# Half of each conditioning block weighed by TensorE, and first operands of two stages loaded one stage ahead

## What the kernel must compute

```python
mod = c @ w_ada[l] + b_ada[l]                  # c: 1 x 1024, w_ada: 1024 x 6144
sh_a, sc_a, gt_a, sh_f, sc_f, gt_f = jnp.split(mod[:, None, :], 6, axis=-1)
h = rmsnorm(x, norm_mix[l]) * (1.0 + sc_a) + sh_a
x = x + gt_a * hybrid_mixer(h, w_in[l], w_conv[l], ...)   # h @ w_in, convolution, gated delta rule, attention
h = rmsnorm(x, norm_ffn[l]) * (1.0 + sc_f) + sh_f
x = x + gt_f * hierarchical_moe(h, ...)
```

## Time and profile before

| | us |
|---|---|
| median of 3 runs | 2518.68 (2518.53 to 2520.19) |
| the profiled execution, its own time | 2507.53 |
| its span in the profile | 2505.4 |
| TensorE busy in the span | 2206.2 (88%) |
| VectorE, ScalarE, GpSimd busy | 1126.5, 922.0, 382.8 |
| mean granted TensorE clock | 0.949 of full speed |

### The profile page before, as it was taken

The page is one execution under the profiler, slowest core; times in us unless marked ns, Lnnn a source line. Parts: engine busy times, 40 slices in busy tenths (PEclk is TensorE's granted clock), DMA queues, the critical chain, the costliest instruction groups (busy, mean ns, idle before and its releaser), DMA issues. The chain is left out here.

```text
span 2505.4 us, 33260 instructions
## 1 busy us (share of the span) xinstructions
PE 2206.2 (88%) x9964; PEld 1242.9 (50%) x9965; DVE 1126.5 (45%) x2294; ACT 922.0 (37%) x2136; POOL 382.8 (15%) x320
## 2 busy tenths in 40 slices
PE   3999899999988897897999998878885998999990
PEld 2666544444444445896777774444552333333330
DVE  5444222232233752555888775656652222222223
ACT  1333111111233311224778774323323443444433
POOL 0000000000011101344333110010012222222220
PEclk9999999999999998998999999988887999999995
DMA  8444102211255544985223324343354988989747
GB/s 341 147 153 147 50 34 90 104 59 50 99 173 178 182 178 131 311 261 200 89 92 105 102 89 162 127 119 99 121 210 148 306 261 284 328 249 312 218 80 287
DMA packets 178320, 418.13 MB, mean 167 GB/s; under 512 B 41192, under 2 KB 81000, under 8 KB 162744
## 3 DMA queue, kind: packets, MB, share of 16 engines
q1 hardware_dynamic: 155944, 346.59, 39.6%
q0 software_dynamic: 13472, 45.26, 7.8%
q10 hardware_dynamic: 8816, 25.18, 2.9%
HBM read 296.84 MB, written 124.85 MB: 168 GB/s over the span
## 5 line engine op out<-in xcount | busy, mean ns | idle before, releaser
L644 PE MATMUL ps<-big,pc_w 128*128 128x512 f32 x1280 | 558.0, 597 | 10.6 <-DMA pc_w<-in_w_chan 10.6
L644 PEld LDWEIGHTS ps<-big,pc_w 128*128 128x128 f32 x1280 | 243.9, 192 | 312.3 <-issue 300.9
L2108 PE MATMUL ps<-big,ex_xt 128*64 x672 | 302.2, 603 | 2.1 <-ACT ex_xt L2151 2.1
L2109 PE MATMUL ps<-ex_wgu,ex_xt 128*64 128x512 f32 x672 | 302.2, 603 | 0.0
L1621 PE MATMUL ps<-w_out,mo_yt 128*128 128x512 f32 x512 | 235.5, 619 | 0.0
L309 PE MATMUL ps<-cp_wt,big 128*128 128x344 f32 x768 | 225.4, 454 | 0.0
L2159 ACT COPY ex_wgu<-big 128x4096 f32 x43 | 155.1, 3607 | 84.7 <-SPq L2025 51.9
L309 PEld LDWEIGHTS ps<-cp_wt,big 128*128 128x128 f32 x768 | 145.8, 191 | 76.9 <-issue 4.0
L1363 PE MATMUL ps<-at_v,at_pt 128*128 128x128 f32 (+1 forms) x1200 | 182.8, 290 | 0.0
L1429 ACT ACTIVATE at_p<-at_p,at_low 128x256 f32<-128x256 f32 (+1 forms) x384 | 174.0, 456 | 19.1 <-DVE at_low L1392 18.8
L2108 PEld LDWEIGHTS ps<-big,ex_xt 128*64 128x64 f32 x672 | 89.7, 139 | 181.1 <-issue 181.1
(11 more groups left out here) (295 smaller groups left out, 3187.8 us busy)
## 6 DMA issues: line engine op xcount, KB each, us to landing
big<-in_w_gate_up SPq DMA_DIRECT2D x32, 2048.0 KB, 11.2
ex_wd<-in_w_down SPq DMA_DIRECT2D x32, 1024.0 KB, 6.6
cp_w<-in_w_ada SPq DMA_DIRECT2D x24, 1024.0 KB, 5.4
ch_d<-pc_cv SPq DMA_DIRECT2D x20, 1024.0 KB, 4.1
at_v<-v_d SPq DMA_DIRECT2D x27, 512.0 KB
o_d<-at_o SPq DMA_DIRECT2D x48, 264.0 KB, 2.1
mo<-o_d SPq DMA_DIRECT2D x16, 792.0 KB
pc_qkv<-ch_d SPq DMA_DIRECT2D x16, 768.0 KB, 5.6
```

Source lines behind the costliest of these rows:

```text
L644: last = nc.tensor.matmul(ps[:, n % 2, :], w[:, ch % 2, k, :], m.ht[:, k, g * BANK:(g + 1) * BANK], start=(k == 0), stop=(k == KD - 1))
L2108: nc.tensor.matmul(ps[0:HB, 2 + b, :], xt[:, b, k, 0:HB], wgu[:, bass.ds(at * WGU + k * 2 * DE, 2 * DE)], start=(k == 0), stop=(k == KD - 1))
L2109: last = nc.tensor.matmul(ps[HB:P, 2 + b, :], xt[:, b, k, HB:P], wgu2[:, b, k, :], start=(k == 0), stop=(k == KD - 1))
```

## The change

TensorE takes over the second half of each of the first four blocks: `c`'s second half is spread over 128 columns (`cb`), and four accumulating matmuls of `cb` with the half's tiles give directly the row that `over_partitions` then adds to. The PSUM bank alternates between blocks. The weight loads of the first projection are waited for pair by pair. The first channel weights move to a tensor that lives through stages 1 and 2 and are loaded in the middle of stage 1. Chunk 0's `nt`, `dz`, `dzt` and `kc` get a place in `mod`'s first 2048 columns (free after stage 1) and are loaded near the end of stage 2.

```diff
+        cb = R.sb("cb", [P, KH, P])
+        chan_in = R.sig("chan_in", 16)
-        c_in, cst_in, wt_in, nrm_in = R.sig("c_in", 16), R.sig("cst_in", 16), R.sig("wt_in", 16), R.sig("nrm_in", 16)
+        c_in, cst_in, wt_in, nrm_in = R.sig("c_in", 16), R.sig("cst_in", 16), S("wt_in", KD // 2, 16), R.sig("nrm_in", 16)
+        def on_pe(n):
+            return n < HALVES * FIRST and n % HALVES == 1
+        def used_up_to(n):
+            return n // HALVES + 1 if n < HALVES * FIRST else n + 1 - FIRST
+        def row_m(n):
+            return ROW_M - n % 2 if n < FIRST else ROW_M
                     if n >= NW:
-                        sp.wait_ge(*w_used.n(n - NW + 1))
+                        if on_pe(n - NW):
+                            sp.wait_ge(*pe_used.n((n - NW) // HALVES + 1))
+                        else:
+                            sp.wait_ge(*w_used.n(used_up_to(n - NW)))
...
                     store(t)
+                    if t == NT // 2:
+                        sp.dma_start(m.w_chan[:, :, :], a["w_chan"][0]).then_inc(*chan_in.inc)
+                sp.wait_ge(*chan_in.n(1))
...
                     pe.wait_ge(*acc_ready.n(n + 1))
-                    pe.wait_ge(*mod_ready.n(n))
-                    nc.tensor.matmul(ps[:, ROW_M, :], m.ones, acc[:, n % 2, :], start=True, stop=True).then_inc(*sum_done.inc)
+                    if n >= FIRST:
+                        pe.wait_ge(*mod_ready.n(n))
+                    nc.tensor.matmul(ps[:, row_m(n), :], m.ones, acc[:, n % 2, :], start=(n >= FIRST), stop=True).then_inc(*sum_done.inc)
+                def second_half(n):
+                    pe.wait_ge(*w_in[(HALVES * n + 1) % NW].n((HALVES * n + 1) // NW + 1))
+                    if n >= 2:
+                        pe.wait_ge(*mod_ready.n(n - 1))
+                    for k in range(KH):
+                        last = nc.tensor.matmul(ps[:, row_m(n), :], cb[:, k, :], w[:, (HALVES * n + 1) % NW, k, :], start=(k == 0), stop=False)
+                    last.then_inc(*pe_used.inc)
...
+                pe.wait_ge(*cb_ready.n(1))
+                second_half(0)
                 pe.wait_ge(*cst_in.n(1))
                 for n in range(FIRST):
+                    if n + 1 < FIRST:
+                        second_half(n + 1)
                     over_partitions(n)
                 turn(0)
-                pe.wait_ge(*wt_in.n(KD // 2))
...
+                            if t == 0 and g == 0 and k % 2 == 0:
+                                pe.wait_ge(*wt_in[k // 2].n(1))
...
+                V.tensor_copy(cb[:, :, :], ct[:, KH:].unsqueeze(2).to_broadcast([P, KH, P])).then_inc(*cb_ready.inc)
                 for blk in range(FIRST):
-                    for half in range(HALVES):
-                        weigh(HALVES * blk + half)
+                    weigh(HALVES * blk)
                     if blk:
                         take_mod(blk - 1)
```

```diff
 # stage 2
-                load_w(0)
+                load_w(1)
...
-                load_w(1)
...
                 store_cv(NCH - 2)
+                first_nt, dz, dzt, kc = m.first
+                sp.wait_ge(*blank.n(2))
+                sp.wait_ge(*nt_out[0].n(1))
+                sp.dma_start(first_nt, m.nt_d[0]).then_inc(*first_in.inc)
+                for k in range(P // SB):
+                    s = slice(k * SB, (k + 1) * SB)
+                    sp.dma_start(h4(dz[s, :])[:, :, s], small_blocks(m.xb_d, 0, k)).then_inc(*first_in.inc)
+                    sp.dma_start(h4(dzt[s, :])[:, :, s], small_blocks(m.xtb_d, 0, k)).then_inc(*first_in.inc)
+                sp.dma_start(h4(kc), m.ch_d[GH:2 * GH, :, 0:P].rearrange("c p n -> p c n")).then_inc(*first_in.inc)
                 store_cv(NCH - 1)
+                sp.wait_ge(*first_in.n(2 + 2 * (P // SB)))
...
+                for k in range(1, 3):
+                    nc.gpsimd.memset(m.first[k], 0.0).then_inc(*blank.inc)
...
-                    pe.wait_ge(*w_in[ch % 2].n(ch // 2 + 1))
+                    if ch:
+                        pe.wait_ge(*w_in[ch % 2].n((ch + 1) // 2))
 # stage 3
                 sp.dma_start(gain[:, :], row_bc(a["gdn_norm"], P)).then_inc(*gain_in.inc)
-                load_solve(0)
                 load_chain(0)
...
-                    pe.wait_ge(*nt_in[b].n(c // 2 + 1))
-                    pe.wait_ge(*d_in[b].n((c // 2 + 1) * BL))
-                    pe.wait_ge(*yy_ready.n(2 * c))
+                    if c:
+                        pe.wait_ge(*nt_in[b].n((c + 1) // 2))
+                        pe.wait_ge(*d_in[b].n((c + 1) // 2 * BL))
+                        pe.wait_ge(*yy_ready.n(2 * c))
 # block_kernel
+        m.first = [m.mod[:, k * GW:(k + 1) * GW] for k in range(4)]
+        with nc.sbuf_tensor("w_chan", [P, KD, P], F32) as m.w_chan:
+            for phase in PHASES[:2]:
+                phase(nc, m, a)
```

More of the change, by code:

```diff
@@ L259, in _ @@
                 for k in range(0, KD, 2):
-                    sp.dma_start(wt[:, k:k + 2, :], a["w_tok"][:, k:k + 2, :]).then_inc(*wt_in.inc)
+                    sp.dma_start(wt[:, k:k + 2, :], a["w_tok"][:, k:k + 2, :]).then_inc(*wt_in[k // 2].inc)
                 load_x(2)
@@ L368, in weigh @@
                     ins.then_inc(*w_used.inc)
-                    dve.wait_ge(*w_used.n(n + 1))
-                    if half == HALVES - 1:
+                    dve.wait_ge(*w_used.n(used_up_to(n)))
+                    if half == HALVES - 1 or n < HALVES * FIRST:
                         dve.sem_inc(*acc_ready.inc)
@@ L437, in pair @@
             return R.sb(name, [P, 2, GW])
-        w = R.sb("w", [P, 2, KD, P])
+        w = (m.w_chan, R.sb("w", [P, KD, P]))
         wc = R.sb("wc", [P, NCONV * CONV])
@@ L475, in project_channels @@
         x_ready = R.sig("x_ready")
+        blank, first_in = R.sig("blank", 1, 0), R.sig("first_in", 16, 0)
         dve_self, act_self = R.plain("dve_self"), R.plain("act_self")
@@ L508, in load_w @@
                         sp.wait_ge(*ch_done.n(GROUPS * (n - 1)))
-                    sp.dma_start(w[:, n % 2, :, :], a["w_chan"][n]).then_inc(*w_in[n % 2].inc)
+                    sp.dma_start(w[n % 2][:, :, :], a["w_chan"][n]).then_inc(*w_in[n % 2].inc)
                 def store_cv(n):
@@ L643, in group @@
                     for k in range(KD):
-                        last = nc.tensor.matmul(ps[:, n % 2, :], w[:, ch % 2, k, :], m.ht[:, k, g * BANK:(g + 1) * BANK], start=(k == 0), stop=(k == KD - 1))
+                        last = nc.tensor.matmul(ps[:, n % 2, :], w[ch % 2][:, k, :], m.ht[:, k, g * BANK:(g + 1) * BANK], start=(k == 0), stop=(k == KD - 1))
                     last.then_inc(*ch_done.inc)
@@ L914, in pair @@
             return R.sb(name, [P, 2, GW])
-        kc, qg, kg, vb, z = pair("kc"), pair("qg"), pair("kg"), pair("vb"), pair("z")
-        nt, aqk, dz, dzt = pair("nt"), pair("aqk"), pair("dz"), pair("dzt")
+        qg, kg, vb, z = pair("qg"), pair("kg"), pair("vb"), pair("z")
+        aqk = pair("aqk")
+        nt, dz, dzt, kc = ((first, R.sb(n, [P, GW])[:, :]) for n, first in zip(("nt", "dz", "dzt", "kc"), m.first))
         yy = pair("yy")
@@ L959, in load_solve @@
                         sp.wait_ge(*y_done.n(2 * (c - 1)))
-                    sp.dma_start(nt[:, b, :], m.nt_d[c]).then_inc(*nt_in[b].inc)
+                    sp.dma_start(nt[b][:, :], m.nt_d[c]).then_inc(*nt_in[b].inc)
                     if c >= 2:
@@ L964, in load_solve @@
                     else:
-                        sp.wait_ge(*zeroed.n(4))
+                        sp.wait_ge(*zeroed.n(2))
                     for k in range(P // SB):
                         s = slice(k * SB, (k + 1) * SB)
-                        sp.dma_start(h4(dz[s, b, :])[:, :, s], small_blocks(m.xb_d, c * GH * P // SB, k)).then_inc(*d_in[b].inc)
-                        sp.dma_start(h4(dzt[s, b, :])[:, :, s], small_blocks(m.xtb_d, c * GH * P // SB, k)).then_inc(*d_in[b].inc)
+                        sp.dma_start(h4(dz[b][s, :])[:, :, s], small_blocks(m.xb_d, c * GH * P // SB, k)).then_inc(*d_in[b].inc)
+                        sp.dma_start(h4(dzt[b][s, :])[:, :, s], small_blocks(m.xtb_d, c * GH * P // SB, k)).then_inc(*d_in[b].inc)
                 def load_chain(c):
@@ L1022, in _ @@
                 link = Chain(pool, pool_self)
-                for b in range(2):
-                    nc.gpsimd.memset(dz[:, b, :], 0.0).then_inc(*zeroed.inc)
-                    nc.gpsimd.memset(dzt[:, b, :], 0.0).then_inc(*zeroed.inc)
+                nc.gpsimd.memset(dz[1][:, :], 0.0).then_inc(*zeroed.inc)
+                nc.gpsimd.memset(dzt[1][:, :], 0.0).then_inc(*zeroed.inc)
                 pool.wait_ge(*gain_in.n(1))
@@ L1054, in fifth_y @@
                     b = c % 2
-                    pe.wait_ge(*nt_in[b].n(c // 2 + 1))
-                    pe.wait_ge(*d_in[b].n((c // 2 + 1) * BL))
-                    pe.wait_ge(*yy_ready.n(2 * c))
-                    heads(Y, nt[:, b, :], dz[:, b, :], y_done)
+                    if c:
```

(14 more changed lines are left out.)

11 lines of the change are left out of this document (5 added, 6 removed).

## The result

The changed kernel takes 2502.8 us (median of 6 runs, 2497.7 to 2507.9) against 2518.6; as a ratio 0.9942, interval 0.9926 to 0.9958, which is 14.6 us less (15.8 by the medians). Forecast were 2501.4 and a range of 2496 to 2511.

What follows compares the result with a forecast made beforehand. TensorE, busy nearly throughout, was taken to bound the kernel, so only its late start and two hand-over holes could give time: 2518.7 less 1.0, 9.5 and 6.8 (17.3) gave 2501.4 us, range 2496 to 2511.

Steps and rivals of the forecast that it cites:

- Start of stage 1: Stage 1 up to the last block taken: TensorE's weighing ends it at 41.6 against 42.59, 1.0 us gained.
- the rows give the clock a longer life than the holes here: Stage 1: TensorE's clock would outlast the waits for DMA, against the Trainium skill's rule on bursts falling back to slow clock.
- mild form of rival 1: Stage 1: slow clock hits only half 3, total gain 13.7, 2505 us; half of rival 1's chance of 0.15.
- The chain itself: Stage 1: each block a round trip TensorE, ones-matmul, VectorE; half 7 issued at 30.1, landing at 34.9; end 41.6.
- Hand-over 1 to 2: Stage 1 to 2: TensorE starts at release, 296.6, without a half-clock stretch; four groups end at 324.6 against 334.11, 9.5 us.
- the bound of 7.0: Hand-over from stage 1 to 2: the gain would be 7.0 us if the clock falls.
- The 0.2 for ScalarE's copy: Stage 2's start: group 2 must wait for ScalarE's copy of group 0, costing 0.2 us.
- Hand-over 2 to 3: Stage 2 to 3: chunk 0's mask 7.0 us earlier, less 0.2 for chunk 1's blocks; 6.8 us, bounds 5 and 8.
- chunk 1's wait: Stage 3: chunk 1's blocks arrive slightly late for `fifth_y(1)`; 0.2 us lost, between 0 and 1.
- The stalls move along: Stage 3, 989 to 1145: TensorE stands 13 us, but loads are issued as chunks finish, so stalls shift with the start.
- The sum: Whole kernel: gains of 1.0, 9.5 and 6.8, together 17.3 us, from 2518.7 to 2501.4 us.
- Signs of being wrong: First block over 3 us later, clock 0.50 after first channel group begins, over 2 us wait for chunk 1, or gain lost by stage 3's end.

Runs made afterwards that it cites:

- dve_weighs: Changed kernel with VectorE weighing both halves of the first blocks again, both early loads kept; 2503.5 us, ratio 0.9942 to the kernel before.
- after_big: Changed kernel with the first eight `w_ada` halves and biases 2 and 3 in places of their own; 2500.6 us, ratio 0.9934 to the kernel before.
- chunk0_late_pieces: Changed kernel with stage 3's large loads in smaller pieces and chunk 0's operands loaded in stage 3 again; 2493.6 us, ratio 0.9916 to the kernel before.
- after_again: The changed kernel run once more without any edit; 2501.9 us, ratio 0.9944 to the kernel before.
- the spread pair: Changed kernel with stage 3's large loads spread in time, chunk 0's operands early or late; 2511.3 and 2516.0 us, ratios 0.9979 and 0.9993 to the kernel before.

## Why the prediction was right, and where it was not

- *Start of stage 1, forecast -1.0*: wrong in sign. The first projection came 1.7 to 1.9 us later. The step that failed is the clock in the pauses: "the rows give the clock a longer life than the holes here". After 963.9 and 293.4 it had fallen 3.7 and 5.1 us into the hole; here it fell 2.0 us after a burst of 5.9 us. Two distances were no bound, as the second trace of the kernel before shows: in the same hole at the end of stage 1 its clock fell 2.5 us after the last matmul. The mild form of rival 1 held for halves 3 and 7: their bursts took 6.05 and 5.15 us where 3.6 stood in the sum. The chain itself (round trip, half 7 issued late, landing 36.8 against 34.9) was right, and dve_weighs and after_big bear it out.
- *Hand-over 1 to 2, forecast 9.5*: measured 8.3 to 8.7. TensorE starts at the release as said; the missing 1 us is the clock again, down in a hole of 3.2 us. It was down for 3.1 us of work and not for 4.9, so the gain stayed above the bound of 7.0 that I had given for this case. In chunk0_late_pieces and after_big it stayed up, and release to fourth copy is 27.8, 9.8 less than before. The 0.2 for ScalarE's copy do not show in the traces: the 64 passes follow each other without a wait.
- *Hand-over 2 to 3, forecast 6.8*: 7.1 at the mask as forecast (7.0); chunk 1's wait is 2.2 instead of 0.2, so 6.0 to 7.0 at chunk 0's copy (in after_again the wait is 1.1).
- *"The stalls move along"*: only in part. By three pairs of times 1 to 5 us of chunk 0's earlier start reach the end; by the spread pair of traces most is given back, with small pieces nothing. Release to TensorE's first pass of attention averages 190.1 us over six traces with the early load and three large bias loads as before, and 193.8 over three with the late load: 3.7 left. Single traces lie up to 4.3 us off these means, so how much of the rest is systematic stays open. What the prediction left out is the size of what stands ahead of the small loads: the same bytes in smaller pieces took about 9 us off.
- *The sum* came within 1.4 us of the median, and that is in part luck. By the mean differences of the table the three places gave 7.2 us (+2.6 - 8.5 - 6.5 + 5.2) and not 17.3: stage 1 missed by 3.6, the first hand-over by 1.0, the chunks of stage 3, which the sum put at nothing, by 5.2, and the second hand-over by 0.3. Outside the sum, the rest of stage 2 came out 5.2 us shorter in the two traces of the changed kernel, by the clock. The medians differ by 15.8, more than the spans of these traces (9.1 on the mean), so the four traces are too few to share out the gain. By the edits undone on the chip: w_chan early 8 to 9, chunk 0 early 4 to 5, TensorE's weighing nothing that times can tell; together 12 to 14 of the 14.6.
- *Signs of being wrong*: two that the prediction had named did come, the clock at 0.50 after the first channel group had begun (until 302.6), and a wait of over 2 us for chunk 1 (2.19 in one trace of two). Neither took the time out of the range.

## What to carry to other kernels

An operand that a stage's first instruction waits for is worth loading a stage ahead where the hole shows in the windows; its worth is the wait plus the clock that the hole costs, less what the next operand is late. Moving work to an idle TensorE in bursts with waits for data between them pays only if the bursts come in time; price each burst at both clock levels. Before counting on a wait to move along, look at what large transfer stands ahead of the small ones it waits for, and cut it into pieces: that was worth 9 to 11 us here, at least as much as the better of the two early loads.

## What the runs showed of the hardware that I had not expected

- TensorE's clock fell 2.0 to 2.7 us after the first burst of stage 1 in eight traces and 4.7 and 4.8 us after it in two; after steady work up to the end of stage 1 in the kernel before it fell after 5.2 us in one trace and after 2.5 in the other. After pauses of 3 us in the start it was up in one execution and down in seven.
- What a fall costs is half of the time at half clock: 0, 3.4, 6.8 and 10.2 us of it in the rest of stage 2 went with some 631.7, 633.2, 635.0 and 636.9 us.
- 1024 KB loads spaced more widely, bias and attention in pairs, made TensorE wait longer for the small loads behind them: its waits went from 16.5 and 19.0 us to 24.1, though the DMA share fell from 0.86 and 0.82 to 0.79; in pieces of 256 and 512 KB they went to 9.8 at a share of 0.90.
- Executions of one kernel on one chip spread by 11 us (2495.4 to 2506.7). The traces show parts of such a spread: the clock's falls in stage 2 (up to 5 us) and the length of stage 5 (up to 8 us).
